# A gate product moved ahead of the transposes and the down product of the pass before it, in a mixture-of-experts stage on TensorE

## The reference, cut to what matters

```python
xb = h[tok_buf].reshape(n_blk, r, d)
def expert_block(args):
    xr, e = args
    return (jax.nn.silu(xr @ w_gate[e]) * (xr @ w_up[e])) @ w_down[e]
yb = lax.map(expert_block, (xb, blk_e)).reshape(cap, d)
return jnp.zeros_like(h).at[tok_buf].add(yb * w_buf[:, None])
```

## Time and profile before

| | us |
|---|---|
| median of 3 runs | 1856.69 (1856.19 to 1856.93) |
| span of the profiled execution | 1854.0 |
| busy in it: TensorE | 1745.3 (94%) |
| busy: VectorE, ScalarE, GpSimd | 810.5, 486.2, 394.9 |
| gate and up products, L2713, without those that read the fourth home | 188.2 |
| down products, L2731, likewise | 107.3 |

### The profile page before, as it was taken

The page is one execution under the profiler, slowest core; times in us unless marked ns, Lnnn a source line. Parts: engine busy times, 40 slices in busy tenths (PEclk is TensorE's granted clock), DMA queues, the critical chain, the costliest instruction groups (busy, mean ns, idle before and its releaser), DMA issues.

```text
span 1854.0 us, 19751 instructions
## 1 busy us (share of the span) xinstructions
PE 1745.3 (94%) x7472; PEld 1027.3 (55%) x7472; DVE 810.5 (44%) x1330; ACT 486.2 (26%) x847; POOL 394.9 (21%) x472
## 2 busy tenths in 40 slices
PE   5999999999999999999999999999898887988887
PEld 2555555555556777677766478885533333333332
DVE  4626555464457556456555687663330000000004
ACT  3221422414233443434443200002321101111012
POOL 2114142240436433444334000000010000010000
PEclk9999999999999999999999999999899998999989
DMA  7221323212321111111113344467679999999996
GB/s 303 95 80 57 114 68 97 76 55 68 103 68 35 46 46 45 45 34 45 45 34 103 125 136 137 135 229 266 272 309 429 430 430 429 429 392 429 430 425 246
DMA packets 153697, 340.17 MB, mean 183 GB/s; under 512 B 15430, under 2 KB 105759, under 8 KB 140826
## 3 DMA queue, kind: packets, MB, share of 16 engines
q1 hardware_dynamic: 135760, 315.26, 44.9%
q10 hardware_dynamic: 13114, 15.89, 2.6%
q0 software_dynamic: 4752, 8.05, 1.1%
HBM read 331.44 MB, written 16.99 MB: 188 GB/s over the span
## 4 chain that ended last, share of the span: by engine, by line
PE 88%; DMA 6%; DVE 3%; issue 2%; ACT 1%; SPq 0%; DVEq 0%; ACTq 0%
PE bank L774 12%; PE bank L522 12%; PE bank L2713 11%; PE bank L1835 10%; PE bank L815 6%; PE bank L2731 6%; PE bank L527 5%; PE bank L518 3%; PE bank L1877 3%; PE bank L1386 3%; DMA stay<-in_w_up_dram 2%; DMA stay<-in_w_down_dram 2%; PE bank L859 2%; DMA arena<-in_w_up_dram 2%; PE bank L867 1%
## 5 line engine op out<-in xcount | busy, mean ns | idle before, releaser
L774 PE MATMUL bank<-stay,arena 128*128 128x512 f32 (+1 forms) x704 | 240.0, 496 | 0.0
L2713 PE MATMUL bank<-arena 128*64 128x512 f32 x832 | 188.2, 609 | 14.3 <-ACT arena L2616 6.2
L774 PEld LDWEIGHTS bank<-stay,arena 128*128 128x128 f32 x704 | 132.4, 190 | 99.7 <-issue 92.3
L522 PE MATMUL bank<-arena 128*128 128x512 f32 x384 | 168.9, 592 | 0.0
L1256 POOL TENSOR_TENSOR arena<-arena 128x256 f32<-128x256 f32 x112 | 87.6, 782 | 269.3 <-DVE arena L1509 155.2
L2713 PEld LDWEIGHTS bank<-arena 128*64 128x64 f32 x832 | 66.4, 140 | 131.4 <-issue 119.1
L2731 PE MATMUL bank<-arena 128*64 128x512 f32 x416 | 107.3, 675 | 32.3 <-issue 18.8
L522 PEld LDWEIGHTS bank<-arena 128*128 128x128 f32 x384 | 71.7, 190 | 83.7 <-issue 83.7
L815 PE MATMUL bank<-arena,stay 128*128 128x512 f32 x256 | 114.6, 595 | 2.2 <-DVE arena L1067 2.2
L2854 DVE TENSOR_TENSOR arena<-arena,bank 128x512 f32<-128x512 f32 x17 | 11.7, 688 | 237.5 <-PE bank L2713 237.5
L1528 DVE TENSOR_TENSOR arena<-arena 128x256 f32<-128x256 f32 x112 | 59.0, 567 | 106.1 <-ACT arena L1287 73.0
(11 more groups left out here) (456 smaller groups left out, 2800.5 us busy)
## 6 DMA issues: line engine op xcount, KB each, us to landing
arena<-in_w_gate_dram SPq DMA_DIRECT2D x24, 2048.0 KB, 18.0
arena<-in_w_down_dram SPq DMA_DIRECT2D x24, 2048.0 KB, 23.3
arena<-in_w_up_dram SPq DMA_DIRECT2D x22, 2048.0 KB, 22.9
arena<-in_w_in_dram SPq DMA_DIRECT2D x58, 512.0 KB, 3.8
arena<-in_w_ada_dram SPq DMA_DIRECT2D x12, 2048.0 KB, 10.5
stay<-in_w_gate_dram SPq DMA_DIRECT2D x8, 2048.0 KB, 22.9
stay<-in_w_up_dram SPq DMA_DIRECT2D x8, 2048.0 KB, 17.2
arena<-in_w_in_dram ACTq DMA_DIRECT2D x6, 2048.0 KB, 9.7
```

What stands on the lines that cost most here:

```text
L522: mm = pe.matmul(b[:, :], w[:, k, :], src[:, k, 0:LAT], start=(k == 0), stop=(k == KT - 1))
L774: mm = pe.matmul(ps[:, 0:n], w[:, k, :], hT[:, k, o:o + n], start=(k == 0), stop=(k == KT - 1))
L2713: mm = pe.matmul(b[cols, :], xgT[r][:, k, cols], w[u][:, k, :], start=(k == 0), stop=(k == KT - 1))
```

## The change

In TensorE's program the gate product of the next pass is issued ahead of this pass's four transposes and its down product, wherever this step and the next are both ordinary ones (steps 0 to 6 and 9 to 12). Its waits go with it. Nothing else is changed: SyncE, ScalarE, VectorE and GpSimd have the programs of before.

```diff
+            def gate_ahead(step):
+                return 0 <= step < STEPS - 1 and TWICE not in (step, step + 1)
+
+            def gate_of(step):
+                p, c = FIRST_PASS[step], 3 * step
+                if p:
+                    pe.wait_ge(s_xgc, p + 1)
+                    pe.wait_ge(s_sig, p)
+                else:
+                    pe.wait_ge(s_ra, FIRST_COLUMNS)
+                up(c, p % 2, landed(c), bank[2], s_g, first=(p == 0))
+
             for step in STEP:
...
+                if not gate_ahead(step - 1):
+                    gate_of(step)
                 if p:
-                    pe.wait_ge(s_xgc, p + 1)
-                    pe.wait_ge(s_sig, p)
                     pe.wait_ge(s_gu, p)
-                else:
-                    pe.wait_ge(s_ra, FIRST_COLUMNS)
-                up(c, r, landed(c), bank[2], s_g, first=(p == 0))
                 up(c + 1, r, landed(c + 1), bank[3], s_u)
                 if p + 1 < PASSES:
                     rows(1 - r, arrived(p + 1), p + 1)
+                if gate_ahead(step):
+                    gate_of(step + 1)
                 if p:
                     pe.wait_ge(s_guc, p)
                 turn_gated(r, p)
```

## The result

The changed kernel takes **1888.55 us** (median of 4 runs, 1887.1 to 1889.64), the kernel before beside it 1856.44. The ratio is 1.0176 with a 95% interval of 1.0162 to 1.0190: slower by 1.8%. The forecast was 1887.

The account below looks back on a forecast made before the run. The DMA queue, if SyncE keeps it filled, was taken to bound the expert stage. Late first down product, nine 32.0 us turns and the passes between sum to 30.7 us late: 1884.7, plus 2.7 for the median, 1887 us; range 1874 to 1899.

Parts of the forecast that it names:

- the double passes: Passes 8 and 9 of the expert stage keep their order, 50.7 us; they end at 1654.0, 19 us late.
- The ring: Moved passes: down product ends, gate load issues and lands, gate product, transposes, copy, next down product; 32.0 us a turn.
- X: Time the moved gate product loses to a slow clock after its idle wait; taken as 1.7 us.
- rival B: Slow stretches after 7 us idle cost 2.8 us each time: 10 us more, 1897 us; chance 0.08.
- The lead: Between gate load issue and use only up product and row transposes remain, some 8 us; the landing takes 14.5.
- The startup gap: Near 1390 us, DMA engines idle 5 us or more; first down product ends at 1390.9 instead of 1383.0.
- What I costed at nothing: Earlier up load, later down load, GpSimd's scatters and gathers, VectorE's multiply and bank 2: cost 0.
- A: The DMA's rate paces all nine turns at 31.1 us: 8 us less, 1879 us; chance 0.15.
- C: Gate product fills TensorE's 3 us wait in 11 passes: 52 us faster, 1805 us; chance 0.03.
- D: Gate load lands within its 8 us plus queue savings: 0 to 8 us late, 1857 to 1865; chance 0.05.
- the floor of 31.1 us: Expert stage: the DMA needs 31.1 us for one pass of weights with gathers and scatters, the lower bound of a turn.

Follow-up runs that it names:

- the run with step 0 alone: Changed kernel with the gate product moved ahead in step 0 only: 1863.19 us, ratio 1.0045 to the kernel before.
- the load in halves: Changed kernel with gate loads of steps 2 to 7 and 10 to 13 cut in two, product starting on the first half: 1870.95 us, ratio 1.0085.
- light loads: Three quarters of each weight load of steps 1 to 13 and the loop left out: kernel before 1835.91 us, changed kernel 1845.26 us.
- steps 9 to 12 alone: Changed kernel with the gate product moved ahead in steps 9 to 12 only: 1863.80 us, ratio 1.0051 to the kernel before.

## Why the prediction was right

**The path.** Each end that the sum names, forecast and measured, in us from the start of the span. In this execution the stage began 0.8 us later (1356.58 against 1355.81).

| end of | forecast | measured |
|---|---|---|
| down(0) | 1390.9 | 1391.8 |
| down(6), six turns | 1582.9 | 1585.7 |
| down(7) | 1603.3 | 1605.7 |
| down(9), the double passes | 1654.0 | 1656.4 |
| down(10) | 1688.9 | 1691.6 |
| down(13), three turns | 1784.9 | 1787.7 |
| up(14) | 1791.8 | 1794.6 |
| span | 1884.7 | 1886.5 |

**The ring.** Forecast 32.0 us a turn; measured 193.9 / 6 = 32.3 on average in the first stretch and 96.1 / 3 = 32.0 in the second. Two terms were slightly off and partly cancel. From the first issue to the start of the gate product I had 14.6 us; the nine measure 13.3 to 16.5 and 14.4 on average. For the gate product with its slow stretch I had 8.6; the nine measure 8.53 to 9.72 and 9.09 on average. X is thus 2.0 against the product's 7.09, not 1.7, and short of the 2.8 of rival B.

The single turns are less even than the sum has them: 31.0, 33.5, 31.1, 34.2, 31.2, 32.9, and then 31.5, 33.5, 31.1 us. This goes with what is unfinished in the queue when the gate load goes out. In four turns the queue was empty by then, or the down load ahead landed within 1.6 us; from the issue of the gate load to the start of its product it was 13.3 to 14.0 us. In four others the down load had 2.5 to 2.9 us to go, and it was 14.5 to 16.5 us. (In the ninth, at 13.9 us, the trace does not show the landing.) For example, the down load issued at 1429.7 landed at 1458.1, 1.6 us after the gate load had gone out at 1456.5, and that one needed 13.3 us; the down load issued at 1463.2 landed at 1490.4, 2.8 us after the gate load of 1487.6, which needed 16.5. So a short turn leaves more of the down load unfinished, and the next turn is long. This is read from one trace; no run was made for it. The prediction had a fixed landing of 14.5, taken from a single pair that went out into an almost empty queue. That this equals the average of nine landings of two kinds is partly luck.

**The lead.** That it is the lead and not the order is shown from both sides: given back, it restores the time (ratio 0.9993), and taken from the old order, it costs 2.9%.

**The startup gap.** Forecast as 5 us or more of idle DMA near 1390: 7.7 us in the 10 of the window. In the sum it is the late end of the first down product, 1390.9 against 1383.0, and the run with step 0 alone prices it at 8 us.

**What I costed at nothing** held. The up load behind the gate load costs nothing that a measurement can tell. The scatters and gathers end no wait of TensorE in the stage. The shift is carried to the end but for 1 us: from the end of up(14) to the end of the span it is 92.9 us before and 91.9 after, as the slow stretches fell differently.

**The rivals.** A, the DMA's rate as the pace of all nine turns, is out for the changed kernel: they average 32.2 us at a share of 0.94 to 0.98. But it lies close: four of the nine single turns take 31.0 to 31.2. It is what happens one step further, with the load in halves. C fails by the row that I held against it: the gate product waits for the same columns, and with light loads the new order is no faster. The Trainium skill's advice (Perfetto Trace Analysis, Matmul Optimizations) to run matmuls back to back in batches did not bear on this stage: before the change the DMA share was 1.01 while TensorE had time to spare. The Trainium skill's fixed cost and rate (DMA: Bandwidth & Descriptors, Anatomy of one DMA), fitted on another issue path, gave an estimate of 11.6 us for a pair; the trace has 13.3 or more in each of the nine turns, and the measurement decides. D is out by the same nine waits.

**Where I was off.** In the sum, no term by more than half a microsecond a turn. Two readings were loose: the earlier trace rows has the next gate product start at 1634.60 and not 1634.8, and the DMA engines stand at nine tenths in the last quarter of the slices of the earlier trace rows, not in the last third. Four expectations missed: the floor of 31.1 us was applied from the first turn of the ring with halved loads, the range for steps 9 to 12 alone took each turn and slow stretch to be those of the changed kernel, and the spans of both light kernels were put too high.

What stays open is why landings with 2.5 to 2.9 us of the load ahead unfinished still range from 14.5 to 16.5 us; no run was made for it.

## What to carry to other kernels

When a product is moved ahead on TensorE, look first at what frees the buffer of its operand: the lead of a load is the work between the product that frees its buffer and the one that uses it, and a move can cut it from three products to one without touching a transfer. Hand out buffers and issue loads in the order of use, and compare each lead with the measured issue-to-landing time, not with bytes over bandwidth. Where the DMA share of a stage is already full, as here, closing a gap of another engine gained nothing, and a single late load cost its full delay.

## What the runs showed of the hardware

After 5.5 to 8.8 us without work, TensorE's next product of 32 instructions took 8.53 to 9.72 us against 7.09 in the changed kernel. Ahead of its gate(4) the granted clock was 1.00 in the first 1.7 us of the wait (1464.3 to 1466.0) and 0.50, the level of 1.2 GHz, at the end of it (1468.0 to 1469.8); it stayed at 0.50 in the product's first 3 us and was 1.00 again from 1474 on. After a wait of 3.05 us it took 7.09 in some passes and 8.4 to 10.05 in others, in the light run of the new order. Ahead of gate(3) there, which took 7.09, the granted clock was 1.00 through the whole wait; ahead of gate(4), which took 8.46, it was 0.86 on average in the wait, and 0.50 in the product's first 2 us (1456 to 1458). A long wait cost no more than a short one could (1.4 to 2.6 us against 0 to 3.0); I had expected 1.7 us after every one.

A pair of 2 MiB weight loads, issued with up to 2.9 us of an earlier load unfinished ahead of it, landed 13.3 to 16.5 us after its first issue, the wake-up of TensorE included.
